# A triangular inverse in a fused two-model kernel: 64x64 blocks against compact 32x32 diagonal blocks

## The chip, the cores and the metric

The kernel runs on 1 core of one Trainium2 chip. It is one program for a whole forward pass; the metric is the device time of one execution in microseconds (us). Its median over three runs is given, and beside it one execution that was profiled.

## The reference, cut to what matters

Two blocks run one after the other on 256 tokens of width 1024: a transformer (two layers) and a recurrent model (two layers of FFN, mixer, FFN). The change lies in the mixer of the second, in the part called RWKV-7:

```python
def step(S, inp):
    r_t, w_t, k_t, v_t, kk_t, b_t = inp
    sa = jnp.einsum('bhvk,bhk->bhv', S, kk_t)
    S = (S * w_t[:, :, None, :]
         - sa[..., :, None] * b_t[:, :, None, :]
         + v_t[..., :, None] * k_t[:, :, None, :])
    return S, jnp.einsum('bhvk,bhk->bhv', S, r_t)
S0 = jnp.zeros((Bn, H, N, N), jnp.float32)
_, ys = lax.scan(step, S0, xs)
```

There are 8 heads of width 64. The kernel does the scan in 4 chunks of 64 tokens. Within a chunk the state's corrections depend on each other through a strictly triangular 64x64 matrix A = (decayed b) times (decayed kk), one for each head and chunk, and what is needed is the inverse of I + A. All of this is float32.

## The kernel before

**Layout.** 8 heads x 4 chunks are 32 small matrices. They lie as 16 units (`UNITS`, four pairs of heads x four chunks) of 64 columns in a tile of 128 partitions x 1024: head h of a pair on partitions 64h to 64h+63. `units(v)` (line 241) is that view. `unit(v, u, h)` is one 64x64 block, and `per_unit(bank, left, right, us)` (lines 2450 to 2455) makes one 64x64 product for each unit and head, into PSUM banks `bank` and `bank + 1`: head 0 uses the array's tile at rows and columns 0 to 63, head 1 the one at 64 to 127.

**The inverse.** `at_` is the masked A transposed, `xs` and `xt` are the growing inverse and its transpose. `xs` and `xt` start as the inverse of 2x2 blocks (masks `low1`, `up1`, then I minus that). Then `LEVELS = [2, 4, 8, 16, 32]` doubles the size of the inverted diagonal blocks five times. A level takes `aoff`, the part of A that joins two neighbouring blocks (mask `lev{m}`, `next_level`, VectorE, line 1701), and on TensorE (lines 2566 to 2580):

```python
per_unit(0, aoff, xs, range(b * 8, b * 8 + 8)).then_inc(lev_p, 1)
for t in gates_at("level", i):
    tile(t, bank=6)
for b in range(2):
    pe.wait_ge(lev_a, LA.at(f"w{b}", step))
    if i < len(LEVELS) - 1:
        per_unit(2, xt, ws, us)
    per_unit(4, ws, xt, us).then_inc(lev_p, 1)
```

The first line is W = A_off X, in two halves of 8 units. ScalarE copies W from PSUM to `ws` (line 1194). X W and its transpose follow, in two halves, and VectorE subtracts them from `xs` and `xt` (line 1817), again by halves. The next level's first half of W waits for the first half's subtraction (`lev_v`), its second half for the second. The last level makes only the product for `xt`, since only `xt` is used afterwards.

**What runs beside it.** `tile(t)` (line 2359) is a column tile of the gate projection: 24 products of 128x128 by 256 columns (lines 2030 to 2032, high and low parts of both operands). `gates_at` places such tiles between the steps: one in each of the first four levels, none in the fifth, then one at the start of each of the four steps of the chunk loop. Its weights come by SP's queue in pairs (`ring_a`, two slots), ScalarE rounds them (`round_t`, line 1012), POOL makes the low part (line 585), and ScalarE empties the result (`empty_gate`, line 1051) and then rounds the tile after next. VectorE does, after each of the first four levels' subtractions, one of four parts of another head normalisation (`standardise`, lines 1799 to 1803).

**Before the inverse.** `per_unit(0, bh, kt)` and `per_unit(2, kt, bh)` (lines 2470, 2471) make A transposed and A in PSUM; VectorE masks them into `at_` and `xs` (`masked`, line 1694), makes `xt` from `at_` (line 1713), and takes both from the identity (lines 1718, 1719). TensorE goes on meanwhile with other products and tiles.

**After it** comes the chunk loop (line 2585 on): for each chunk a product `r` (`sums`, line 2594), a gate tile, the product with `xt` ("u"), VectorE's negation of it (`nu`, line 1875), then state and output. TensorE enters the loop when VectorE has subtracted the last half of `xt`.

The order on each engine is written out by hand, as above; nothing is planned by costs.

## Time and profile before

| | us |
|---|---|
| median of three runs | 2489.09 (2487.69 to 2493.08) |
| profiled execution, its own time | 2488.33 |
| its span, first to last instruction | 2485.8 |
| TensorE busy (matmul) | 2369.6, 95% of the span |
| VectorE, ScalarE, POOL busy | 1449.3, 1047.2, 319.3 |
| mean granted TensorE clock | 0.98 of full speed |

The two layers' inverses lie at 1438.7 to 1481.4 us and 2149.0 to 2191.6 us of the span. TensorE's busy share counts overlapping matmuls once. A clock of 1.00 is 2.4 GHz, 0.50 is 1.2 GHz.

### The profile page before, as it was taken

To read this page: it belongs to the slowest core of one execution; us is meant where nothing else is said; L and a number is where in the kernel's file an instruction comes from. 1 tells how busy PE (TensorE), PEld (TensorE's weight loads), DVE (VectorE), ACT (ScalarE), POOL (GpSimd) and SP (SyncE) were. 2 spreads that over 40 slices of the span, in tenths; PEclk is the share of its full clock that TensorE was granted. 3 is DMA by queue.
4 is the path that set the end of the run, shared out by engine and by line. 5 is a ranking of instruction groups with operands and counts; after the bars stand their busy time and mean duration, and the time that the engine had idled before them with its cause. 6 is when DMAs were issued, how large, how long until landed. Compare 5 with 4: busy or idle time off the path is not lost.

```text
span 2485.8 us, 47529 instructions
## 1 busy us (share of the span) xinstructions
PE 2369.6 (95%) x19164; PEld 2095.1 (84%) x19164; DVE 1449.3 (58%) x2314; ACT 1047.2 (42%) x1666; POOL 319.3 (13%) x263
## 2 busy tenths in 40 slices
PE   7988999999998799999999999999999999999998
PEld 3755899999985599879988888899899888988997
DVE  1053266656625276676667765566666668555665
ACT  3154454454335343343346434433433355435333
POOL 0000000000000000010014435300100125336000
PEclk9999999999999899999999999999999999999999
DMA  6255454544425454355433223654455232124542
GB/s 267 71 198 216 178 191 176 189 169 176 169 85 219 154 203 179 150 178 190 177 106 123 81 72 125 220 189 177 154 189 190 102 138 100 69 87 178 201 179 102
DMA packets 65512, 392.51 MB, mean 158 GB/s; under 512 B 7264, under 2 KB 7392, under 8 KB 28000
## 3 DMA queue, kind: packets, MB, share of 16 engines
q1 hardware_dynamic: 64224, 383.81, 42.3%
q10 hardware_dynamic: 864, 5.16, 0.5%
q8 instruction: 104, 1.70, 0.3%
q0 software_dynamic: 288, 1.57, 0.2%
q14 instruction: 32, 0.26, 0.0%
HBM read 389.46 MB, written 1.05 MB: 157 GB/s over the span
## 4 chain that ended last, share of the span: by engine, by line
PE 82%; DVE 4%; POOL 4%; issue 4%; ACT 3%; DMA 2%; POOLq 0%; SPq 0%; DVEq 0%; ACTq 0%
PE ps L2048 19%; PE ps L2030 11%; PE ps L2031 11%; PE ps L2032 11%; PE ps L2050 10%; PE ps L2139 6%; POOL t_lo L585 3%; PE ps L2154 2%; PE ps L2453 2%; DMA ring_a<-in_wa 2%; PE ps L2594 1%; POOL h_parts L563 1%; PE ps L2000 1%; PE ps L1977 1%; PE ps L2169 1%
## 5 line engine op out<-in xcount | busy, mean ns | idle before, releaser
L2048 PE MATMUL ps<-h_parts,w_hi 128*128 128x512 f32 x2080 | 742.1, 399 | 4.8 <-DVE mod L1258 2.9
L2050 PE MATMUL ps<-h_parts,w_lo 128*128 128x256 f32 x2080 | 584.9, 281 | 0.0
L2048 PEld LDWEIGHTS ps<-h_parts,w_hi 128*128 128x128 f32 x2080 | 391.9, 188 | 96.7 <-DVE mod L1258 3.2
L2050 PEld LDWEIGHTS ps<-h_parts,w_lo 128*128 128x128 f32 x2080 | 394.1, 189 | 0.1
L1330 DVE TENSOR_TENSOR w_lo<-ring_a,w_hi 128x1024 fp32r<-128x1024 f32 x308 | 366.5, 1232 | 24.7 <-ACT w_hi L679 24.5
L2030 PE MATMUL ps<-hid_hi,d_hi 128*128 128x256 f32 x1232 | 349.0, 283 | 0.0
L2031 PE MATMUL ps<-hid_lo,d_hi 128*128 128x256 f32 x1232 | 348.8, 283 | 0.0
L2032 PE MATMUL ps<-hid_hi,d_lo 128*128 128x256 f32 x1232 | 348.6, 283 | 0.0
L711 ACT ACTIVATE sg<-sg 128x256 f32<-128x256 f32 x130 | 54.3, 418 | 655.5 <-DVE sg L1366 655.5
L679 ACT CAST w_hi<-ring_a 128x1024 fp32r<-128x1024 f32 x308 | 305.6, 1040 | 12.3 <-DMA ring_a<-in_wa 12.3
L2030 PE MATMUL ps<-h_parts,t_hi 128*128 128x256 f32 x880 | 260.8, 296 | 17.4 <-POOL t_lo L585 10.6
L1366 DVE TENSOR_REDUCE sg<-ps 128x256 f32<-128x512 f32 x130 | 89.9, 692 | 302.4 <-PE ps L2050 302.4
L2031 PE MATMUL ps<-h_parts,t_hi 128*128 128x256 f32 x880 | 252.8, 287 | 0.0
L2032 PE MATMUL ps<-h_parts,t_lo 128*128 128x256 f32 x880 | 252.5, 287 | 0.0
L563 POOL TENSOR_TENSOR h_parts<-nsq,h_parts 128x256 fp32r<-128x256 f32 x72 | 61.4, 876 | 1435.1 <-ACT h_parts L698 849.3
L2030 PEld LDWEIGHTS ps<-hid_hi,d_hi 128*128 128x128 f32 x1232 | 234.2, 190 | 6.0
L2032 PEld LDWEIGHTS ps<-hid_hi,d_lo 128*128 128x128 f32 x1232 | 234.6, 190 | 0.0
L2031 PEld LDWEIGHTS ps<-hid_lo,d_hi 128*128 128x128 f32 x1232 | 234.5, 190 | 0.0
L585 POOL TENSOR_TENSOR t_lo<-ring_a,t_hi 128x512 fp32r<-128x512 f32 x120 | 172.7, 1463 | 314.6 <-ACT t_hi L1012 314.6
L1337 DVE TENSOR_TENSOR d_lo<-ring_d,d_hi 128x1024 fp32r<-128x1024 f32 x154 | 190.1, 1235 | 11.5 <-ACT d_hi L687 8.9
L2030 PEld LDWEIGHTS ps<-h_parts,t_hi 128*128 128x128 f32 x880 | 172.2, 196 | 25.9 <-issue 13.6
L2031 PEld LDWEIGHTS ps<-h_parts,t_hi 128*128 128x128 f32 x880 | 173.0, 197 | 0.1
(317 smaller groups left out, 3811.7 us busy)
## 6 DMA issues: line engine op xcount, KB each, us to landing
ring_a<-in_wa SPq DMA_DIRECT2D x282, 1024.0 KB, 4.8
ring_d<-in_wd SPq DMA_DIRECT2D x154, 512.0 KB, 5.2
work<-in_wa SPq DMA_DIRECT2D x6, 1024.0 KB, 22.1
work<-in_small POOLq DMA_DIRECT2D x2, 768.0 KB, 5.7
c<-in_c ACTq DMA_DIRECT2D x1, 1175.0 KB, 10.8
work<-in_c ACTq DMA_DIRECT2D x1, 1088.0 KB, 5.0
x<-in_x ACTq DMA_DIRECT2D x1, 1024.0 KB, 15.2
work<-in_ctx ACTq DMA_DIRECT2D x1, 1024.0 KB, 19.6
```

Of the source, the lines that this page charges most:

```text
L563: nc.gpsimd.tensor_tensor(h_lo[:, k, :], nsq[:, k, :], h_hi[:, k, :].bitcast(F32), ALU.subtract)\
L585: nc.gpsimd.tensor_tensor(t_lo[:, t % 2, k], ring_a[:, c % 2, t % 2, k], t_hi[:, t % 2, k].bitcast(F32), ALU.subtract).then_inc(done, 1)
L679: nc.scalar.copy(w_hi[:, f % 2, part], ring_a[:, c % 2, part]).then_inc(hi_a, 1)
L1330: ins = nc.vector.tensor_tensor(w_lo[:, f % 2, part], ring_a[:, c % 2, part], w_hi[:, f % 2, part].bitcast(F32), ALU.subtract)
L1337: nc.vector.tensor_tensor(d_lo[:, f % 2], ring_d[:, d % 2], d_hi[:, f % 2].bitcast(F32), ALU.subtract)\
L1366: nc.vector.reduce_sum(sg[:, f % 2, :], both_parts(bank), AX_X).then_inc(gate_summed, 1)
L2030: nc.tensor.matmul(out, hi, to_hi, start=start, stop=False, skip_group_check=True)
L2031: nc.tensor.matmul(out, hi, to_lo, start=False, stop=False, skip_group_check=True)
L2032: return nc.tensor.matmul(out, lo, to_hi, start=False, stop=stop, skip_group_check=True)
L2048: nc.tensor.matmul(out, w_hi[:, f % 2, part, k, :], h_parts[:, k], start=(k == 0), stop=False, skip_group_check=True)
L2050: mm = nc.tensor.matmul(out[:, 1, :], w_lo[:, f % 2, part, k, :], h_hi[:, k, :], start=False, stop=(k == KD - 1), skip_group_check=True)
L2139: mm = nc.tensor.matmul(ps[:, 4 + p % 2, 0:cols.stop - cols.start], ring_a[:, slot, i % 2, k, :], h[:, k, cols], start=(k == 0), stop=(k = ...
```

## The change

The diagonal blocks of up to 32x32 are now kept compact: 32 partitions x 32 columns for each unit and each quarter of the partitions, so `xs`, `xt`, `aoff` and `ws` use 512 columns instead of 1024 (`xs_h`, `xt_h`, `off_h`, `ws_h`). Four levels (2, 4, 8, 16) run on these, with four 32x32 tiles of the array on its diagonal (`per_half`). The fifth is replaced by one step for the block that lies off the diagonal: `at_far` times `xs_h`, copied by ScalarE, times the far half of `xt`, negated by VectorE (`far_half`, twice). The gate tile of level 16 moves between these two products. The two products before the inverse are split in 32-wide pieces: the diagonal ones for both (`products_near`) and the far one for A transposed only (`products_far`). VectorE's masks shrink; pieces of `xt` are put back in the 64-wide layout after level 16, and `standardise(3)` comes after them. The constants lose 192 of 2,350 columns.

```diff
-LEVELS = [2, 4, 8, 16, 32]
+LEVELS = [2, 4, 8, 16]
+HALF = CHUNK // 2
...
+        def halves_of(v, first):
+            flat = v[:, first:first + 2, :].rearrange("p j t -> p (j t)")
+            return flat.rearrange("p (u t) -> p u t", t=HALF)
+
+        at_h, at_far, xs_h = halves_of(at_, 0), halves_of(at_, 2), halves_of(xs, 0)
+        off_h, xt_h, ws_h = halves_of(aoff, 0), halves_of(xt, 0), halves_of(ws, 0)
...
 ScalarE, levels:
-                        nc.scalar.copy(units(ws)[:, half * 8:half * 8 + 8, :],
-                                       ps[:, half, :].rearrange("p (u t) -> p u t", t=CHUNK)).then_inc(lev_a, 1)
-                    for t in gates_at("level", i):
-                        empty_gate(t)
+                        nc.scalar.copy(ws_h[:, half * 8:half * 8 + 8, :],
+                                       ps[:, half, 0:T].rearrange("p (u t) -> p u t", t=HALF)).then_inc(lev_a, 1)
+                    if i < len(LEVELS) - 1:
+                        empty_gate(gates_at("level", i)[0])
+                act.wait_ge(far_w, l + 1)
+                for h in range(2):
+                    low = slice(h * CHUNK + HALF, (h + 1) * CHUNK)
+                    ins = nc.scalar.copy(ws_h[low], ps[low, 0, :].rearrange("p (u t) -> p u t", t=HALF))
+                ins.then_inc(far_copied, 1)
+                empty_gate(gates_at("level", len(LEVELS) - 1)[0])
...
 VectorE, before the levels:
-                masked(at_, 0, "strict").then_inc(rw_v, 1)
+                masked_half(at_h, 0, "strict_half")
+                for h in range(2):
+                    high = slice(h * CHUNK, h * CHUNK + HALF)
+                    ins = nc.vector.tensor_copy(at_far[high].rearrange("p (b u) t -> p b u t", b=2),
+                                                ps[high, 0:2, T:2 * T].rearrange("p b (u t) -> p b u t", t=HALF))
+                ins.then_inc(rw_v, 1)
                 dve.wait_ge(rw_p, RP.at("a", l))
-                masked(xs, 2, "low1").then_inc(rw_v, 1)
+                masked_half(xs_h, 2, "low1").then_inc(rw_v, 1)
...
+                for h in range(2):
+                    nc.vector.memset(units(xt)[h * CHUNK + HALF:(h + 1) * CHUNK, :, 0:HALF], 0.0)
+                nc.vector.tensor_tensor(xt_h, at_h, each_half("up1"), ALU.mult).then_inc(rw_v, 1)
...
 VectorE, levels:
-                        for buf, bank in ((xs, 2), (xt, 4))[i == len(LEVELS) - 1:]:
+                        for buf, bank in ((xs_h, 2), (xt_h, 4))[:1 if i == len(LEVELS) - 1 else 2]:
                             ins = nc.vector.tensor_tensor(
-                                units(buf)[:, us, :], units(buf)[:, us, :],
-                                ps[:, bank + half, :].rearrange("p (u t) -> p u t", t=CHUNK), ALU.subtract)
+                                buf[:, us, :], buf[:, us, :],
+                                ps[:, bank + half, 0:T].rearrange("p (u t) -> p u t", t=HALF), ALU.subtract)
                         ins.then_inc(lev_v, 1)
+                    if i == len(LEVELS) - 1:
+                        for b in (1, 0):
+                            for h in range(2):
+                                rows = slice(h * CHUNK + b * HALF, h * CHUNK + (b + 1) * HALF)
+                                split = lambda v: v.rearrange("p (b u) t -> p b u t", b=2)
+                                ins = nc.vector.tensor_tensor(
+                                    split(units(xt)[rows, :, b * HALF:(b + 1) * HALF]), split(xt_h[rows]),
+                                    ps[rows, 4:6, 0:T].rearrange("p b (u t) -> p b u t", t=HALF), ALU.subtract)
+                            if b:
+                                ins.then_inc(near_xt, 1)
+                        dve.wait_ge(far_x, l + 1)
+                        for h in range(2):
+                            rows = slice(h * CHUNK, h * CHUNK + HALF)
+                            ins = nc.vector.tensor_scalar(units(xt)[rows, :, HALF:CHUNK],
+                                                          ps[rows, 1, :].rearrange("p (u t) -> p u t", t=HALF),
+                                                          -1.0, None, ALU.mult)
+                        ins.then_inc(xt_whole, 1)
...
 TensorE, before the levels:
+                def products_near(bank, left, right):
+                    for u in range(UNITS):
+                        for h in range(2):
+                            for b in range(2):
+                                row = h * CHUNK + b * HALF
+                                mm = nc.tensor.matmul(ps[row:row + HALF, bank + u // 8, u % 8 * HALF:(u % 8 + 1) * HALF],
+                                                      near(left, u, h, b), near(right, u, h, b), start=True, stop=True,
+                                                      tile_position=(h * HD, row))
+                    return mm
...
-                per_unit(0, bh, kt).then_inc(rw_p, 1)
-                per_unit(2, kt, bh).then_inc(rw_p, 1)
+                products_near(0, bh, kt)
+                products_far(0, bh, kt).then_inc(rw_p, 1)
+                products_near(2, kt, bh).then_inc(rw_p, 1)
...
 TensorE, levels:
+                def per_half(bank, left, right, us):
+                    for u in us:
+                        for g in range(4):
+                            row = slice(g * HALF, (g + 1) * HALF)
+                            mm = nc.tensor.matmul(ps[row, bank + u // 8, u % 8 * HALF:(u % 8 + 1) * HALF],
+                                                  left[row, u, :], right[row, u, :], start=True, stop=True,
+                                                  tile_position=(g * HALF, g * HALF))
+                    return mm
+                def far_half(bank, left, right, to, back):
+                    for u in range(UNITS):
+                        for h in range(2):
+                            k, m = h * CHUNK + back * HALF, h * CHUNK + to * HALF
+                            mm = nc.tensor.matmul(ps[m:m + HALF, bank, u * HALF:(u + 1) * HALF],
+                                                  left[k:k + HALF, u, :], right[k:k + HALF, u, :], start=True, stop=True,
+                                                  tile_position=(k, m))
+                    return mm
...
-                        per_unit(0, aoff, xs, range(b * 8, b * 8 + 8)).then_inc(lev_p, 1)
-                    for t in gates_at("level", i):
-                        tile(t, bank=6)
+                        per_half(0, off_h, xs_h, range(b * 8, b * 8 + 8)).then_inc(lev_p, 1)
+                    if i < len(LEVELS) - 1:
+                        tile(gates_at("level", i)[0], bank=6)
...
-                        if i < len(LEVELS) - 1:
-                            per_unit(2, xt, ws, us)
-                        per_unit(4, ws, xt, us).then_inc(lev_p, 1)
+                        per_half(2, xt_h, ws_h, us)
+                        per_half(4, ws_h, xt_h, us).then_inc(lev_p, 1)
                 pe.wait_ge(lev_v, LV.at("x1", l * len(LEVELS) + len(LEVELS) - 1))
+                far_half(0, at_far, xs_h, 1, 0).then_inc(far_w, 1)
+                tile(gates_at("level", len(LEVELS) - 1)[0], bank=6)
+                pe.wait_ge(far_copied, l + 1)
+                pe.wait_ge(near_xt, l + 1)
+                far_half(1, ws_h, units(xt)[:, :, HALF:CHUNK], 0, 1).then_inc(far_x, 1)
+                pe.wait_ge(xt_whole, l + 1)
```

## Rows read from the trace of the kernel before

**Rows 1.** The page: busy time, and the chain that ended last, by engine
```profile
PE 2369.6 (95%) x19164; PEld 2095.1 (84%) x19164; DVE 1449.3 (58%) x2314; ACT 1047.2 (42%) x1666; POOL 319.3 (13%) x263
...
PE 82%; DVE 4%; POOL 4%; issue 4%; ACT 3%; DMA 2%; POOLq 0%; SPq 0%; DVEq 0%; ACTq 0%
```

**Rows 2.** Windows: length, busy (records) of PE, PEld, DVE, ACT, POOL; PEclk, DMA, GB/s
```profile
1357.95:1361.83 3.88, 3.88 (x129) 3.81 (x128) 3.88 (x3) 3.53 (x6) 3.88 (x2) 1.00 0.02 4
...
1438.69:1481.37 42.68, 40.04 (x994) 38.55 (x993) 26.45 (x35) 15.28 (x22) 12.29 (x10) 1.00 0.18 67
2148.97:2191.64 42.67, 40.03 (x993) 38.54 (x992) 26.45 (x35) 15.28 (x22) 12.30 (x10) 1.00 0.18 65
```

**Rows 3.** Chain of waits, layer 0's inverse: start us, us, what
```profile
1447.76 1.30 DVE work L1817 x2
...
1449.10 1.15 PE ps L2453 x32
1450.24 0.32 PE ps L2030
...
1453.31 3.90 PE ps L2453 x128
...
1458.57 1.15 PE ps L2453 x32
...
1469.20 0.32 PE ps L2030
...
1481.37 0.68 PE ps L2594 x16
```

**Rows 4.** TensorE's timeline: column strips, whole array, 64x64 tiles
```profile
844.01 1.93 PE L1977 MATMUL ps<-ring_a,cs 128*32 128x256 f32 x32
...
1436.87 1.89 PE L2562 MATMUL ps<-work,c 128*128 128x256 f32 x8
...
1443.76 4.88 PE L2453 MATMUL ps<-work 64*64 64x64 f32 x160
```

**Rows 5.** Groups by line: busy us, mean ns of one, idle before
```profile
L1786 DVE TENSOR_TENSOR work<-ps,work 128x256 f32<-128x256 f32 x8 | 3.4, 424 | 0.3
L1194 ACT COPY work<-ps 128x512 f32<-128x512 f32 x20 | 11.5, 586 | 35.8 <-PE ps L2453 35.8
L1012 ACT CAST t_hi<-ring_a 128x1024 fp32r<-128x1024 f32 x94 | 98.0, 1043 | 0.0
```

**Rows 6.** Timeline of VectorE, ScalarE and POOL, layer 0
```profile
1445.44 2.50 POOL L585 TENSOR_TENSOR t_lo<-ring_a,t_hi 128x512 fp32r<-128x512 f32 x2 [4.48 <-ACT t_hi L1012]
...
1453.34 0.38 ACT L1051 ACTIVATE work<-ps 128x256 f32<-128x256 f32 x1 [2.46 <-PE ps L2032]
...
1477.39 1.75 DVE L1799 RECIPROCAL work<-work 128x256 f32<-128x256 f32 x1
1479.17 0.42 DVE L1801 TENSOR_TENSOR work<-work 128x256 f32<-128x256 f32 x1
1479.63 0.49 DVE L1803 SCALAR_TENSOR_TENSOR work<-work,vec 128x256 f32<-128x256 f32 x1
...
1481.50 1.55 DVE L1867 SCALAR_TENSOR_TENSOR work<-work,vec 128x256 f32<-128x256 f32 x4
1485.78 0.42 DVE L1875 TENSOR_SCALAR work<-ps 128x256 f32<-128x256 f32 x1 [2.73 <-PE ps L2594]
```

**Rows 7.** Windows around a drop of the granted clock, layer 0, before the inverse
```profile
1400.40:1406.10 5.70, 5.70 (x17) 4.50 (x17) 1.67 (x3) 4.09 (x6) 0.00 (x0) 0.50 0.00 0
1406.10:1410.10 4.00, 4.00 (x26) 4.00 (x26) 0.56 (x1) 0.00 (x0) 0.00 (x0) 0.69 0.00 0
```

**Rows 8.** The page's DMA parts, and one of TensorE's waits
```profile
q8 instruction: 104, 1.70, 0.3%
...
ring_a<-in_wa SPq DMA_DIRECT2D x282, 1024.0 KB, 4.8
...
PE ps L1977 <- DMA c<-in_c: 3.1, 1, 3.1
```

More of the change, by code:

```diff
@@ L477, in gates_at @@
         def gates_at(what, i):
-            if what == "level" and i == len(LEVELS) - 1:
-                return []
             return [GATES + dict(head=0, mean=4, level=6, chunk=10, y=14)[what] + i]
@@ L2468, in _, with near @@
                     tile(25)
+                def near(v, u, h, b):
+                    j, c = u // NC_, u % NC_
+                    at = c * CHUNK + b * HALF
+                    return v[h * HD:h * HD + HD, j, at:at + HALF]
+                def products_near(bank, left, right):
[7 more added lines that the diff above has]
+                    return mm
@@ new lines, in products_far @@
+                def products_far(bank, left, right):
+                    for u in range(UNITS):
+                        for h in range(2):
+                            row, col = h * CHUNK, T + u % 8 * HALF
+                            mm = nc.tensor.matmul(ps[row:row + HALF, bank + u // 8, col:col + HALF],
+                                                  near(left, u, h, 0), near(right, u, h, 1), start=True, stop=True,
+                                                  tile_position=(h * HD, row))
+                    return mm
```

37 lines of the change are left out of this document (23 added, 14 removed).

## The prediction

> **What bounds the kernel now.** I read the page first. TensorE is busy 95% of the span and carries 82% of the chain that ended last; no other engine has more than 4% of that chain [rows 1]. So what the change takes from TensorE counts, if nothing else ends last in its place. The stretches by window then give the size of the stage: the triangular inverse, from its first product to the first product of the chunk loop, takes 42.68 us in layer 0 and 42.67 in layer 1, with the clock at 1.00 [rows 2]. That is 85.35 us, 3.4% of the span; all else in the diff lies in the 3.88 us of the two products before it. Last I read the chain of waits inside the stage [rows 3]. It repeats: X and XT products (128 records, 3.90 us), the two subtractions of VectorE (1.30), the second half of the next W (32 records, 1.15), one 128x128 gate tile (1450.24 to 1453.31, 3.07), and again, each 9.47 us after the last. The first half of W hides under the subtractions.
>
> **Price of a record.** An f32 product leaves two records: per unit and head one product, so 64 records for 32 products. 160 records of 64 columns take 4.88 us [rows 4], 29.3 ns each once the tail of the last is taken off (4.88 - 0.22 over 159). Two tiles of the array alternate, so each tile takes 58.6 ns for a record. Do tiles really run beside each other? 32 records of 256 columns in four column strips take 1.93 us, and 8 records of the same 256 columns on the whole array take 1.89 [rows 4]: four strips cost what one costs, 216 ns a round ((1.93 - 0.4) / 7). From 256 to 64 columns a tile's record falls by 0.82 ns a column, so at 32 columns it costs 32.4 ns, and with four tiles at once 8.1 ns. That is the low bound. The high bound is 29.3 ns, the fastest that the trace shows records going in over a long burst; nothing shows that records can be fed faster than that for long. I take 9 ns: near the low bound, since the strips show fourfold overlap with the same f32 records, with 10% for start-up and supply. Where only two tiles can work (the products that cross from one half block to the other) I take 16 ns.
>
> The Trainium skill, "TensorEngine Tiling (Array Packing)", section Instruction Overhead, speaks against the change: a small matmul has about 60 cycles of overhead, and one should not tile a dimension that is already small. That would be 25 ns a record if the overhead is the array's. The strips of [rows 4] are too long to show it.
>
> **Records.** Before, the inverse has 96 products on each of four levels and 64 on the fifth: 448, or 896 records a layer. After: four levels of 64 + 64 + 64 products, and two crossing steps of 32: 1,536 records on four tiles and 128 on two. So it has 1.9 times the records at, by my price, under a third of the cost. The two products before the stage go from 128 records to 256 on four tiles and 64 on two.
>
> **The level period after.** W 128 x 9 = 1.15 us; X and XT 256 x 9 = 2.30; the gate tile with its switch 3.17; start-ups 0.1. Then the wait for VectorE: result 0.24, two subtractions. These halve to 256 elements. Such VectorE instructions take 0.42 us, and four in a row 1.55 [rows 5, 6], so two take 0.83 where two of 512 took 1.30; with the release 1.12. The first half of W (0.58) runs inside it, 0.54 is exposed. Period 7.25 against 9.47: 2.2 saved, three times, 6.65. The first W, before the first gate tile, is 128 x 9 = 1.2 for 64 x 29.3 = 1.9 with 0.1 of start: 0.8 saved.
>
> **The end of the stage.** Before: gate tile at 1469.20 to chunk loop at 1481.37, 12.17 us [rows 3]. After, from where that tile would stand: X and XT 2.34; result and one subtraction (xs alone is waited for) 0.71; first crossing step 64 x 16 = 1.05; the moved gate tile 3.17; second crossing step and its result 1.29; two VectorE negations of 512 elements from PSUM, which now end the stage with nothing beside them, 1.33 (two L1817 in 1.30). Sum 9.89: 2.3 saved. ScalarE's two copies of the crossing step (0.59 each, L1194) start when that step ends and are done 1.3 us later, under the tile of 3.1. VectorE's four pieces of xt (4 x 0.61) start with the first crossing step and last 2.5, also under step and tile. Without the tile both would be bare: it is the cover that the move buys. Behind the new waits stand: on TensorE the second crossing step and the chunk loop; on ScalarE the emptying of that gate tile, due 3 us later; on VectorE the negations and all of the next paragraph.
>
> **Moved past queues.** In VectorE's order one of the four parts of the head normalisation stands behind each level: 2.65 us (1.75 + 0.42 + 0.48). With a mask, now of half width (some 0.65), and four subtractions (1.7) that makes 5.0 in a period of 7.25, so VectorE is not the bound. The fourth part used to run at 1477.39 beside TensorE and now stands behind the negations, so it runs as the chunk loop opens: 2.7 + memset + the four of L1867 (1.55) = 4.6 us, and the first nu, which TensorE waits for, came 4.4 us into the loop (1485.78) [rows 6]. I charge 0.35. POOL and ScalarE prepare the gate tiles: 0.38 + 1.04 + 2.50 = 3.9 us after a tile ends the one after next is ready [rows 5, 6]; with periods of 7.25 there are 11 us. The moves of SP's queue are none; a pair of tiles needs one load, 4.8 us to landing, in 14.5 us [rows 8].
>
> **The front.** 128 x 29.3 = 3.8 becomes 256 x 9 + 64 x 16 = 3.3: 0.5 saved. The masks shrink, but two partition-sliced copies of 512 elements come before the release of "at": about 0.6 later than now, and TensorE asks for it 0.5 earlier; that gap is covered by a tile and transposes of 4.1 us except some 0.2. Bounds 0 and 0.6; 0.3 taken. The constants shrink by 192 columns (96 KB) and TensorE waits 3.1 us for that load [rows 8]: 0 to 0.3 us a run, 0.2 taken.
>
> **Sum.** 6.65 + 0.8 + 2.3 - 0.35 + 0.3 = 9.7 a layer, 19.4 for two, with the constants 19.6. Profiled execution 2488.33 - 19.6 = 2468.7; the median of the runs, 2489.09, is 0.8 above it: 2469. Each ns on the price of a record costs some 960 + 256 + 128 + 320 = 1,660 records a layer: 3.3 us for both. At 8.1 ns the time is 2466; the gain is gone at 15 ns.
>
> **Rivals.**
>
> A, supply (the other side): a record is a weight load and a product, so a layer gets 960 x 2 = 1,920 more instructions to feed. If TensorE's queue is fed with one record in 20 ns or more, tiles idle between records. Place: every burst of the levels; it decides from 15 ns. At 22 ns, 13 x 3.3 = 43 more: about 2512, with 2505 at 20 and 2536 at 29.3. For it: no long burst beats 29.3. Against: 58.6 ns is what one tile needs for 64 columns (0.82 a column and some 6 over), so that rate has its own cause, and fetching instructions takes 0.3% of the DMA engines [rows 8]. Chance 0.11.
>
> A2, a fixed cost of each record on the whole array, whatever its columns: same place, same bounds (15 to 29.3 ns), same 2512. Against it, four strips of 256 columns cost no more than one record; for it, they are long enough to hide such a cost. Chance 0.10. By the page named above, whose figure is 25 ns, the time would be about 2522.
>
> B, half supply: bursts start full and then run at 11 to 14 ns (fetches of 16 KB among them). 2476 to 2486. Chance 0.13.
>
> C, the clock: in a stretch where TensorE had gone idle now and then and ran matmuls on 4 rows, the granted clock was 0.50 for 5.7 us, and the next gate tile got it back only midway [rows 7]. After the change a quarter of the array works in the bursts, and waits of 0.5 to 1.6 us follow. If it drops at the end of each stage, tile and crossing steps cost 3 to 4 us more a layer: 2476. Against: with half the array and waits of 0.45 it stays at 1.00 now. Chance 0.10.
>
> D, the array does not overlap row tiles that write one bank, or the waits eat it: no change, 2487 to 2491. The alternation of two tiles in one bank speaks against. Chance 0.04.
>
> Forecast, 2462 to 2475: 0.52.
>
> **Chances.** Two kernels within 0.2% (5 us) can't be told apart here. Faster: 0.52 + 0.09 of B and 0.09 of C and a little from between, 0.71; same 0.08; slower 0.21. The range reaches from 2461 (low bound of the price, front in full) to 2502, and leaves out most of A.
>
> **What would show it.** Bursts of 64 records in 0.6 to 0.8 us; 256 of X and XT in 2.3 (right), 3.8 (the gain is gone), 6 (A). Level period 7.2. Stage 33 us (42.7 less 9.75). Clock 1.00 in it. The gate tile of the last level covers ScalarE's copies. Wait of TensorE for the negations 1.3. First nu 4.7 us into the loop. The forecast is wrong if a four-tile burst costs over 12 ns a record, or if the clock leaves 1.00.

## The result, and the profile after

The kernel got slower: 2547.21 us (median of 4, 2544.61 to 2551.01) against 2491.09 us for the kernel before beside it (2487.69 to 2493.79). The ratio is 1.0226, with a 95% interval of 1.0210 to 1.0243. The forecast was 2469, and its range ended at 2502.

The page after: busy time, the instruction queue (packets, MB, share), and the chain that ended last.

```profile
PE 2383.6 (94%) x21084; PEld 2102.0 (82%) x21084; DVE 1438.4 (56%) x2324; ACT 1044.6 (41%) x1666; POOL 317.5 (12%) x263
...
q8 instruction: 119, 1.95, 0.3%
...
PE 82%; issue 6%; POOL 4%; DVE 4%; ACT 3%; DMA 2%; POOLq 0%; SPq 0%; DVEq 0%; ACTq 0%
```

Beside [rows 1] TensorE has 1,920 records more and only 14 us more busy time, but "issue" (TensorE waits for nothing that the profile shows) rose from 4% to 6% of the chain. Beside [rows 8] the instruction queue has 15 packets more. A record is a weight load and a product: 1,920 records are 3,840 instructions, and 3,840 / 15 = 256 to a packet of 16 KB.

Windows after: the front (from the first product for the triangular matrix to the two products on 4 rows) in layer 0 and 1, and the stage in layer 0 and 1. Columns as in [rows 2].

```profile
1367.36:1394.04 26.68, 23.00 (x601) 22.11 (x601) 19.28 (x23) 9.16 (x16) 11.77 (x7) 0.87 0.21 74
2107.10:2135.21 28.11, 22.94 (x603) 21.96 (x603) 16.05 (x22) 9.38 (x16) 10.67 (x8) 0.88 0.30 107
1454.02:1517.00 62.98, 39.56 (x1761) 37.30 (x1760) 20.07 (x33) 13.55 (x22) 10.93 (x9) 0.73 0.13 46
2191.10:2253.63 62.53, 40.58 (x1761) 38.02 (x1760) 20.07 (x33) 13.78 (x22) 11.05 (x9) 0.73 0.13 46
```

And the front before, in the same two layers:

```profile
1357.95:1378.69 20.74, 20.74 (x410) 20.07 (x409) 20.22 (x19) 9.16 (x16) 12.36 (x7) 1.00 0.27 92
2073.60:2094.35 20.75, 20.75 (x409) 19.95 (x407) 17.04 (x18) 9.29 (x16) 11.72 (x8) 1.00 0.38 142
```

The stage was 42.7 us [rows 2]: it grew by 20.3 and 19.9, the fronts by 5.9 and 7.4. That is 53.5 of the 62.7 us between the two profiled executions (2551.01 and 2488.33). The other 9 stand ahead of the changed levels and products: layer 0's front starts at 1367.36 in place of 1357.95. Two kernels further down, with the same text up to there, start it at 1352.4 (the looped one) and 1353.6 (the one with the 64x64 front), so it is a matter of the execution.

One line of the change, as it is printed ahead, differs from the kernel: `xt_h` is `halves_of(aoff, 2)`, the second half of `aoff`'s buffer, so that its pieces can be put into `xt` without writing over what is still to be read.

TensorE's timeline after, inside the first two levels (start, length, what, idle before and its releaser); pieces of the gate tiles are left out.

```profile
1454.02 1.31 PE L2543 MATMUL ps<-work 32*32 32x32 f32 x128
...
1463.37 1.30 PE L2543 MATMUL ps<-work 32*32 32x32 f32 x123 [2.67 <-issue]
1464.93 0.25 PE L2543 MATMUL ps<-work 32*32 32x32 f32 x4 [0.26 <-DVE work L1844]
1469.69 1.07 PE L2543 MATMUL ps<-work 32*32 32x32 f32 x60 [4.51 <-issue]
...
1471.49 0.41 PE L2074 MATMUL ps<-h_parts,t_hi 128*128 128x256 f32 x1
...
1475.93 1.68 PE L2543 MATMUL ps<-work 32*32 32x32 f32 x172
1479.64 0.54 PE L2543 MATMUL ps<-work 32*32 32x32 f32 x40 [2.03 <-issue]
```

The waits of TensorE in the stage of layer 0 after (total, times, longest), and the same view of before:

```profile
PE ps L2543 <- issue: 19.7, 8, 4.5
PE ps L2553 <- issue: 1.1, 1, 1.1
```

```profile
PE ps L2453 <- DVE work L1817: 1.8, 4, 0.5
```

Read together: a burst runs at 10 ns a record while it runs (128 in 1.31, 123 in 1.30, 172 in 1.68), as forecast. But nine times in the stage of layer 0 TensorE stops in the middle of a burst with no semaphore due, for 20.8 us in all (layer 1: 19.7). Before, no wait for issue stands in the view. Between two stops lie 127 or 128 records, one packet of 256 instructions, or twice that where a gate tile lies between (60 + 24 + 172 records).

The trace also has the start of every packet of the instruction queue. In both layers' fronts and stages TensorE stops 23 times for 0.6 us or more. Each time it goes on 2.2 to 2.7 us after a packet has started. And the next packet starts only after TensorE has gone on into the new block: 1.1 to 1.7 us after in 19 of the 23 cases, 2.7 to 4.2 us in four. So one block is asked for when the block before it is begun, and not earlier, and two blocks can't begin closer than some 1.1 + 2.2 = 3.3 us. The closest pair in a stage is 1479.64 and 1482.96, 3.3 us apart.

And then the clock: the records of a gate tile, 0.28 us each at the upper level (granted 1.00, 2.4 GHz), last 0.41 here, at the lower one (1.2 GHz), and the granted clock of the stage is 0.73, a mixture of both.

These two account for the stage: 42.7, less the forecast gain of 9.7, plus 20.8 of stops, makes 53.8; the 9.2 left to 63.0 are the clock's share. That last term is a remainder. Some 6 us of it can be read: three of the four gate tiles take 5.2, 5.3 and 4.6 us from their start to that of the next burst, for 3.05 before.

### The profile page after: what moved, and what is told of

The parts are those of the page before. It is cut to its first block, busy times and chain, and to the rows that moved or that the text cites. A ratio compares the mean times of both kernels' runs of the same rounds, so it can differ in the third digit from the quotient of the medians.

```text
span 2549.1 us, 51379 instructions
## 1 busy us (share of the span) xinstructions
PE 2383.6 (94%) x21084; PEld 2102.0 (82%) x21084; DVE 1438.4 (56%) x2324; ACT 1044.6 (41%) x1666; POOL 317.5 (12%) x263
## 4 chain that ended last, share of the span: by engine, by line
PE 82%; issue 6%; POOL 4%; DVE 4%; ACT 3%; DMA 2%; POOLq 0%; SPq 0%; DVEq 0%; ACTq 0%
PE ps L2092 19%; PE ps L2074 11%; PE ps L2076 11%; PE ps L2075 11%; PE ps L2094 9%; PE ps L2183 5%; POOL t_lo L595 3%; PE ps L2198 2%; PE ps L2543 1%; PE ps L2690 1%; POOL h_parts L573 1%; DMA ring_a<-in_wa 1%; PE ps L2021 1%; PE ps L2044 1%; PE ps L2213 1%
## 5 line engine op out<-in xcount | busy, mean ns | idle before, releaser
L2074 PE MATMUL ps<-h_parts,t_hi 128*128 128x256 f32 x880 | 267.8, 304 | 18.5 <-POOL t_lo L595 10.7
L2076 PE MATMUL ps<-h_parts,t_lo 128*128 128x256 f32 x880 | 258.7, 294 | 1.4 <-issue 1.4
L2075 PE MATMUL ps<-h_parts,t_hi 128*128 128x256 f32 x880 | 259.2, 295 | 0.0
L2074 PEld LDWEIGHTS ps<-h_parts,t_hi 128*128 128x128 f32 x880 | 179.7, 204 | 28.1 <-issue 15.2
L2075 PEld LDWEIGHTS ps<-h_parts,t_hi 128*128 128x128 f32 x880 | 180.0, 205 | 0.1
```

The costliest lines, as they stand in the source:

```text
L2074: nc.tensor.matmul(out, hi, to_hi, start=start, stop=False, skip_group_check=True)
L2075: nc.tensor.matmul(out, hi, to_lo, start=False, stop=False, skip_group_check=True)
L2076: return nc.tensor.matmul(out, lo, to_hi, start=False, stop=stop, skip_group_check=True)
```

## Experiments

Theory 1 (supply): TensorE's instructions come in blocks of 256 by the instruction queue, and a block takes at least 3.35 us to be there (the two closest packets in the first stage of after start 3.36 us apart). Theory 2 (the array): the small products cost more than 9 ns once many follow. Theory 3 (the clock): it falls first and makes the rest.

### The same products from fewer instructions

```diff
+ def twice_over(us, *products):
+     us = list(us)
+     with pe.Fori(0, 2):
+         for bank, left, right in products:
+             per_half(bank, left, right, us[0:3])
+     for bank, left, right in products:
+         mm = per_half(bank, left, right, us[6:8])
...
- per_half(0, off_h, xs_h, range(b * 8, b * 8 + 8)).then_inc(lev_p, 1)
+ twice_over(range(b * 8, b * 8 + 8), (0, off_h, xs_h)).then_inc(lev_p, 1)
...
- per_half(2, xt_h, ws_h, us)
- per_half(4, ws_h, xt_h, us).then_inc(lev_p, 1)
+ twice_over(us, (2, xt_h, ws_h), (4, ws_h, xt_h)).then_inc(lev_p, 1)
```

The kernel leaves out units 3 to 5 of each half and does units 0 to 2 twice.

> The kernel after, with each burst of the four levels run as a loop that passes twice over the products of three units, with the products of the last two units behind it. As many products as before (8 units to a burst, the same shapes, the same four tiles of the array), but fewer different instructions to bring in: about 546 in place of 830 to a level. Units 3 to 5 of each half are left out (others are done twice), so the inverse isn't the reference's. Theory 1 (supply: PE runs out at every 256th instruction and a block of 256 takes at least 3.35 us to come): 546 instructions are 2.1 blocks, 7.1 us, about the period that was forecast for a level, so a level takes 7.5 to 9 us (four loops to a level may cost 0.1 to 0.3 us each), the stage 34 to 39 us in place of 63, the clock in it goes back to 1.00, and the kernel takes 2470 to 2490 us. Theory 2 (the array: 32x32 products on four tiles cost more than 9 ns in a row of levels): the same products, so the stage stays at 63 us and the kernel at 2547. Theory 3 (the clock falls because of the small products themselves, and that makes the stage long): the clock stays at 0.73 in the stage, the stage above 50 us, the kernel above 2525.

Measured: 2513.49 us, 1.0103 (1.0075 to 1.0131) of before; 34 us below after (31 by the two ratios) with the same 21,084 records. That is over theory 1's range and under theory 3's. Nine instruction packets fewer than after. Windows: up to the second level's first subtraction, the whole stage of layer 0, the stage of layer 1. Then TensorE's waits in the stage of layer 0, and VectorE's subtractions.

```profile
1439.24:1455.05 15.81, 15.10 (x706) 13.30 (x705) 5.37 (x10) 8.37 (x12) 5.13 (x5) 1.00 0.34 108
...
1439.24:1488.06 48.82, 41.16 (x1762) 36.55 (x1761) 19.19 (x33) 13.65 (x22) 10.94 (x9) 0.86 0.18 59
2162.73:2215.63 52.90, 42.45 (x1761) 38.22 (x1760) 19.26 (x33) 13.71 (x22) 10.99 (x9) 0.77 0.15 53
```

```profile
PE ps L2543 <- issue: 3.9, 4, 1.7
PE ps L2699 <- DVE work L1861: 1.5, 1, 1.5
```

```profile
1446.29 0.75 DVE L1844 TENSOR_TENSOR work<-work,ps 128x256 f32<-128x256 f32 x2 [4.11 <-PE ps L2543]
...
1455.05 0.75 DVE L1844 TENSOR_TENSOR work<-work,ps 128x256 f32<-128x256 f32 x2 [3.14 <-PE ps L2543]
```

Stops fell from 20.8 to 3.9 us and the stage by 14.2 in layer 0, from 19.7 to 7.2 and by 9.6 in layer 1: theory 2 is out, since the array has the same to do. The first period is 8.76 us (1446.29 to 1455.05), at a clock of 1.00 and with no stop. A W of 128 records takes 2.18 us here in place of 1.31: 0.43 for each of its two loops. A level has four loops, 1.74 us; without them it would be 7.0, and the forecast said 7.25. So with supply, the forecast's working holds. But the stage was expected at 34 to 39 us and took 49 and 53. Loops account for some 7 of that, stops for 4 and 7, and the clock fell to 0.86 and 0.77 with few stops left.

### Twice the columns, the same instructions

```diff
- mm = nc.tensor.matmul(ps[row, bank + u // 8, u % 8 * HALF:(u % 8 + 1) * HALF],
-                       left[row, u, :], right[row, u, :],
+ mm = nc.tensor.matmul(ps[row, bank + u // 8, u % 8 * HALF:(u % 8 + 2) * HALF].rearrange("p (a t) -> p a t", t=HALF),
+                       left[row, u, :], right[row, u, :][:, None, :].to_broadcast([HALF, 2, HALF]),
                        start=True, stop=True, tile_position=(g * HALF, g * HALF))
```

> The kernel after, with 64 moving columns in place of 32 in every product of the levels (the 32 columns given twice; the second copy lands where the next unit's product overwrites it). The same number of instructions, twice the columns. Theory 1 (supply): a block of 256 instructions is 128 records; even at the 14.7 ns a record that 64 columns would take over four tiles it is worked off in 1.9 us, less than the 3.35 us in which a block comes, so the stage stays within 3 us of 63 and the kernel within 6 us of 2547. Theory 2 (the array is the bound): 5 to 6 ns more for each of 1536 records of a layer, 8 to 9 us a layer, so the kernel takes 2563 or more.

Measured: 2540.21 us, 1.0211 (1.0182 to 1.0240), which overlaps after's 1.0226 (1.0210 to 1.0243). Windows of the two stages, and a burst between stops:

```profile
1440.89:1499.40 58.51, 43.91 (x1762) 41.08 (x1761) 19.30 (x33) 13.64 (x22) 10.95 (x9) 0.88 0.14 49
2177.11:2236.36 59.25, 41.94 (x1761) 39.03 (x1761) 19.36 (x33) 13.64 (x22) 10.94 (x9) 0.94 0.13 49
```

```profile
1445.87 2.98 PE L2543 MATMUL ps<-work 32*32 32x64 f32 x197
1450.30 2.23 PE L2543 MATMUL ps<-work 32*32 32x64 f32 x127 [1.46 <-issue]
```

A record now takes 15 ns (2.98 / 197), and the stage is not longer but 3.3 to 4.5 us shorter, at a clock of 0.88 and 0.94. The array's time isn't the bound. Theory 1 had the stage within 3 us of 63, so it is missed a little, on the side away from theory 2. The stops are shorter (12.6 and 15.4 us for 20.8 and 19.7), as they must be if a block comes at a fixed pace while its records take longer. That the clock would be higher stood in neither theory.

### The loops, with twice the columns

Its edit is the two above together, with the same units left out.

> The kernel with the bursts of the levels as loops that pass twice (fewer different instructions, three units of each half left out and others done twice, so the inverse isn't the reference's), and 64 moving columns in each product of the levels in place of 32. Same instructions, same loops, more array time: 5 ns for each of 1536 records, 7 to 8 us a layer. Theory C1 (the granted clock falls where the products are small in columns, with or without stops of PE; in the looped kernel it fell to 0.86 and 0.77 over the stage with few stops, and to 0.56 over a burst without any in the padded one): the clock of the stage goes up to 0.93 to 1.00, and the longer products are paid back: the stage takes 45 to 52 us, about what it took (49 and 53). Theory C2 (the clock falls because PE stops for instructions, whatever it runs in between): the clock stays at 0.77 to 0.86, and the stage is 7 to 9 us longer than with 32 columns, 56 to 62 us.

Measured: 2506.06 us, 1.0071 (1.0056 to 1.0086).

```profile
1444.37:1490.55 46.18, 42.11 (x1762) 38.56 (x1761) 19.09 (x33) 13.64 (x22) 10.94 (x9) 0.96 0.18 62
2160.35:2210.63 50.28, 43.19 (x1761) 39.55 (x1760) 19.19 (x33) 13.65 (x22) 10.96 (x9) 0.93 0.16 57
```

With the products 50% longer the stage is 2.6 us shorter than in the looped kernel with 32 columns, at 0.96 and 0.93 for 0.86 and 0.77. C2's 56 to 62 us are out, and C1's stage of 45 to 52 us is what came. The stops are shorter too, 2.0 and 4.8 us for 3.9 and 7.2, so the columns aren't all that changed.

### Extra instructions in the kernel before

```diff
  pe.wait_ge(lev_a, LA.at(f"w{b}", step))
+ for _ in range(1):
+     for d in range(96):
+         row = slice(d % 4 * 32, (d % 4 + 1) * 32)
+         nc.tensor.matmul(ps[row, 2 + b, 0:2], const("ident")[row, 0:32], const("ident")[row, 0:2],
+                          start=True, stop=True, tile_position=(row.start, row.start))
```

> The kernel before, with 96 extra products of 2 columns in a straight line ahead of each half of the products for X and its transpose, in levels 0 to 4 of a layer (they write a bank that is overwritten right after; 32 rows, 32 columns of weights, spread over the four tiles; constant operands). Each is 2 records and 4 instructions: 768 more to a level beside some 440. Theory 1 (supply): 1208 instructions are 4.7 blocks of 256, at 3.35 us or more each 15.8 us to a level in place of 9.5: at least 51 us more over the ten levels of both layers (levels 0 to 3; the last one has no gate tile and the same padding, so rather 60 to 70), and more if the clock falls: 2540 to 2590 us. Theory 2 (each record has its price on the array and nothing else counts): 3840 more records of 8 to 10 ns, 31 to 38 us more, 2520 to 2530 us.

The second kernel has `with pe.Fori(0, 2)` over 48 of them:

> As the kernel with 96 extra products ahead of each half, but the 96 are 48 in a loop that passes twice. The same products are executed, and 384 instructions fewer are to be brought in for a level (824, 3.2 blocks, 10.8 us at 3.35 us each, which is less than the 12.6 us or so that the level then takes on the array). Theory 1 (supply): 31 to 38 us over the kernel before for the extra records, and up to 5 for the loops: 2522 to 2535 us, at least 15 us less than the one in a straight line. Theory 2 (a record has its price on the array): the same time as in a straight line within 5 us.

The third has 24 in place of 96:

> The kernel before with 24 extra products of 2 columns ahead of each half of X and its transpose, a quarter of the 96 that cost 109 us. 192 instructions more to a level: 632, 2.5 blocks of 256, 8.3 us at 3.35 each, and the level then lasts some 10.4 us, so the blocks come in time. Theory 1 (supply with a threshold): no stop of PE in the levels, only 960 records more at 10 ns: 8 to 13 us over the kernel before, 2498 to 2503. Theory 2 (an added record costs the same whatever the number, 109 / 4): 27 us more, 2517. Theory 3 (the clock: small products lower it at any dose): the clock of the stage below 0.95 and 15 us more or above.

Measured: 2598.77 us in a straight line (1.0437, 1.0410 to 1.0464), 2557.44 looped (1.0281, 1.0252 to 1.0310), 2504.40 with 24 (1.0066, 1.0042 to 1.0090). TensorE's timeline in the straight line of 96:

```profile
1451.12 1.96 PE L2453 MATMUL ps<-work 64*64 64x64 f32 x59 [1.77 <-issue]
1453.02 0.74 PE L2581 MATMUL ps<-c 32*32 32x2 f32 x69
1454.86 1.19 PE L2581 MATMUL ps<-c 32*32 32x2 f32 x123 [1.10 <-issue]
1455.98 0.41 PE L2453 MATMUL ps<-work 64*64 64x64 f32 x5
1458.59 1.65 PE L2453 MATMUL ps<-work 64*64 64x64 f32 x26 [2.20 <-issue]
```

59 + 69 and 123 + 5 records: 128 each, whatever their kind, and they start 3.74 and 3.73 us after one another. That is the rate of supply here, 29 ns a record; the shortest distance seen, the 3.3 us in the stage of after, is 26. The whole is over theory 1's 2540 to 2590 as well. TensorE waits for issue for 18.8 us in the stage of layer 0. The looped kernel executes the same 23,004 records with 15 packets fewer and is 41 us faster: theory 1, and the array's price is out as the reason for the stops. Its waits for issue in the stage of layer 0 sum to 1.1 us. Yet it is 68 us over before, where 31 to 38 were expected. Its windows (both stages, then a padding burst with the X products behind it), and the timeline there:

```profile
1434.81:1508.23 73.42, 69.31 (x2914) 65.42 (x2913) 26.65 (x35) 15.27 (x22) 12.24 (x10) 0.86 0.12 40
...
1445.21:1454.26 9.05, 9.05 (x323) 8.89 (x321) 3.78 (x5) 0.58 (x1) 0.00 (x0) 0.57 0.33 117
```

```profile
1445.21 2.89 PE L2581 MATMUL ps<-c 32*32 32x2 f32 x192
1448.04 6.22 PE L2453 MATMUL ps<-work 64*64 64x64 f32 x128
```

TensorE is busy without a break for 9.05 us, and the granted clock is 0.57. 128 records of X and its transpose, 3.90 us in [rows 3], take 6.22. The clock fell to its lower level at 1442.8, in the burst behind two runs of small products with one stop of 0.31 us between them, and came back at 1453.1. So it can be down where TensorE doesn't stop; what makes it fall isn't shown. Theory 3 names a second cause and not the first, since the straight line loses 41 us more with the same products.

With 24, two stops (0.8 us) stand in the stage of layer 0, the clock is 1.00, and the stage takes 49.86 us. It cost 16.6 us over before (2487.84 beside it): somewhat over theory 1's 8 to 13, which had no stop, and well under the 27 of a price that stays the same. An added record costs 17 ns with 24 products and 28 with 96. So the cost rises faster than the dose, as it does when the blocks come in time at first and then don't.

### The front as it was

```diff
...
- products_near(0, bh, kt)
- products_far(0, bh, kt).then_inc(rw_p, 1)
- products_near(2, kt, bh).then_inc(rw_p, 1)
+ per_unit(0, bh, kt).then_inc(rw_p, 1)
+ per_unit(2, kt, bh).then_inc(rw_p, 1)
...
+ for g in range(4):
+     rows, col = slice(g * HALF, (g + 1) * HALF), g % 2 * HALF
+     ins = nc.vector.tensor_tensor(
+         dst[rows].rearrange("p (b u) t -> p b u t", b=2),
+         ps[rows, bank:bank + 2, :].rearrange("p b (u t) -> p b u t", t=CHUNK)[:, :, :, col:col + HALF],
+         const(mask)[rows, None, None, :].to_broadcast([HALF, 2, 8, HALF]), ALU.mult)
```

> The kernel after with the products in front of the levels as they were (64x64 blocks, two of the array's tiles, 64 products of each kind) and the compact blocks cut out of the bank by VectorE, with four instructions of 32 partitions in place of one of 128 for each of the two masks. 384 instructions fewer for PE in a layer, some 4 us more for VectorE. Theory 1 (supply, also ahead of the levels: two stops of PE, 1.9 and 2.2 us, stand there in the trace of after, and that stretch takes 26.7 us in place of 20.7): the stops go, the granted clock of the stretch is back at 1.00, and since VectorE was busy for 20.2 of 20.7 us before, the stretch is as long as VectorE makes it: 22 to 25 us; the stage of the levels stays at 59 to 63 us; the kernel takes 2533 to 2545. Rival (the six microseconds come from the order of VectorE's work in the new front): the stretch is no shorter than 26 us and the kernel takes 2547 or more.

Measured: 2527.05 us, 1.0163 (1.0144 to 1.0183).

```profile
1353.60:1375.90 22.30, 20.88 (x410) 20.10 (x410) 21.75 (x25) 9.19 (x16) 11.82 (x7) 1.00 0.23 79
2087.40:2108.10 20.70, 20.70 (x409) 20.05 (x408) 19.23 (x27) 9.12 (x16) 11.28 (x8) 1.00 0.39 137
1434.83:1494.91 60.08, 38.91 (x1761) 36.37 (x1760) 20.06 (x33) 13.54 (x22) 10.93 (x9) 0.74 0.14 49
2162.95:2227.60 64.65, 40.23 (x1761) 37.63 (x1760) 20.07 (x33) 13.63 (x22) 10.94 (x9) 0.71 0.13 44
```

The fronts lose their stops (2.0 and 1.7 us in layer 0 of after) and are back at 1.00: 4.4 and 7.4 us shorter. The stages stay long (their sum is 124.7 us for 125.5). The fronts explain 12 us. By the two ratios the kernel gained 16, and their intervals leave that uncertain by some 5, so nothing else has to be found. (The medians alone are 20 apart, and the kernel lies below the 2533 that was expected, but they were taken beside different runs of before.)

### The off-diagonal step alone

The kernel before, levels 2 to 16 as they were, level 32 as in the change:

```diff
+ far_half(0, units(at_)[:, :, HALF:CHUNK], units(xs)[:, :, 0:HALF], 1, 0).then_inc(far_w, 1)
+ tile(gates_at("level", len(LEVELS) - 1)[0], bank=6)
...
+ far_half(1, units(ws)[:, :, 0:HALF], units(xt)[:, :, HALF:CHUNK], 0, 1).then_inc(far_x, 1)
```

> The kernel before with one part of the change alone: the levels 2 to 16 stay in 64x64 blocks on two tiles, and level 32 is the off-diagonal step (product of 32x32 quadrants, copy under the gate tile that is moved there, second product, negated copy). The number of PE's instructions stays about the same (a product of level 32 for a product of the step). Worked out from the rows of before: the level of 16 loses its gate tile (3.1 us) and gains a wait for ScalarE's copy of 1 us, the step has 64 records at 16 ns, the tile, 64 records, and 1.4 us for the negations, and the stage ends within 0.5 us of where it ended. Theory 1 (supply is the only thing that failed): 2489 us within 4, no stop of PE in the stage. Rival (the step has a wait of its own that the forecast missed): 5 us more or worse for both layers.

Measured: 2489.68 us, 0.9998 (0.9984 to 1.0013): no difference. The stages take 41.92 and 41.90 us, with no stop. This part does what it was meant to and, alone, is worth nothing that can be measured.

### Versions meant to beat both

First, 64x64 weights with 32 moving columns for W and X:

```diff
- per_unit(0, aoff, xs, range(b * 8, b * 8 + 8)).then_inc(lev_p, 1)
+ compact(0, aoff, xs_c, range(b * 8, b * 8 + 8)).then_inc(lev_p, 1)
...
  tile(gates_at("level", i)[0], bank=6)
...
+     mm = compact(2, xt, ws_c, range(b * 8, b * 8 + 8))
+ mm.then_inc(lev_p, 1)
+ pe.wait_ge(ws_wide, step + 1)
+ per_unit(4, ws, xt).then_inc(lev_p, 1)
...
  pe.wait_ge(ch_a, step + 1)
+ if c == 0:
+     pe.wait_ge(xt_whole, l + 1)
  sums(narrow(1), [(here(xt), here(rr))]).then_inc(ch_p, 1)
```

> A version meant to beat both: built on the kernel before. The weights stay 64x64 blocks with zeros beside the two 32x32 blocks, so the number of products and of PE's instructions stays as before (64 for W, 64 records each), but the moving operand of W and of X is compact (32 columns), the transposed product keeps 64. ScalarE writes W twice, compact and wide, under the gate tile; level 32 is the off-diagonal step, its negations covered by the first sums and the gate tile of the chunk loop; the whole inverse is computed. Theory 1 (with the supply as before, the array's time counts, and half the moving columns are half of it): W 64 records 1.05 us in place of 1.9, X the same, transposed product 1.9: a level in 7.1 us in place of 9.5, the stage 32 to 36 us in place of 42.7, the kernel 2468 to 2478 us; no stop of PE on a 256th instruction. Rival A (loading 64x64 weights sets the price, not the columns that move): W and X stay at 29 ns a record, the stage 38 to 41 us for the covered negations and the shorter subtractions alone, 2482 to 2488. Rival B (the clock: fewer columns in the levels, and it falls below 0.9 in the stage): stage 38 to 46 us, 2480 to 2500.

Measured: 2483.14 us, 0.9985 (0.9972 to 0.9997): 0.15% faster than before, just clear of the noise.

```profile
1457.30 2.05 PE L2508 MATMUL ps<-work 64*64 64x32 f32 x64
1459.18 2.06 PE L2488 MATMUL ps<-work 64*64 64x64 f32 x64
```

```profile
1443.07:1482.34 39.27, 37.81 (x993) 36.78 (x992) 21.25 (x27) 22.43 (x38) 12.25 (x10) 1.00 0.21 73
```

Half the moving columns take the same 2.05 us, and stage (39.27 in both layers) and time lie where rival A has them; theory 1 is out. With 64x64 weights the moving columns don't set a record's price at this size; I take it that the load does. What is left is the order: both halves of X first, then both of its transpose, and the negations under the chunk loop's first work. It gives 42.68 - 39.27 = 3.4 us a stage, 6.8 for two, and the medians differ by 6.8. The second version keeps that order with all operands wide (edit against the first version, with VectorE's and ScalarE's part left out):

```diff
- compact(0, aoff, xs_c, range(b * 8, b * 8 + 8)).then_inc(lev_p, 1)
+ per_unit(0, aoff, xs, range(b * 8, b * 8 + 8)).then_inc(lev_p, 1)
...
- mm = compact(2, xt, ws_c, range(b * 8, b * 8 + 8))
+ mm = per_unit(2, xt, ws, range(b * 8, b * 8 + 8))
```

> A simpler version meant to beat both: 64x64 blocks throughout as in the kernel before, all operands wide (64 moving columns), with the order of the kernel with compact moving operands: both halves of X first, then both of the transposed product, so that the subtraction for the next W runs beside the transposed product; a gate tile in each of the four levels; level 32 as the off-diagonal step; its negations covered by the first sums and the gate tile of the chunk loop. Theory (the moving columns cost nothing: W's 64 records took 2.06 us with 32 of them and 1.93 with 64, and what made the kernel with compact operands faster is its order alone): the stage 38.5 to 40 us in place of 42.7, the kernel 2480 to 2486. Rival (half of the moving columns did give a part): 2486 to 2490.

Measured: 2486.56 us, 0.9987 (0.9970 to 1.0003), stages of 39.12 and 39.67 us: as short as with compact operands, so the order made the gain in the stage. The whole kernel can't be told from before, nor from the first version: the ratios are 0.9987 and 0.9985, and most of the 3.4 us between the two medians lies between the kernels before that ran beside them (2487.84 and 2489.97). The third puts W of the first version on four tiles:

```diff
- compact(0, aoff, xs_c, range(b * 8, b * 8 + 8)).then_inc(lev_p, 1)
+ quarters(0, aoff, xs_c, range(b * 8, b * 8 + 8)).then_inc(lev_p, 1)
```

> The kernel with compact moving operands, with W alone on four tiles: 32x32 weights, 128 products of it to a level in place of the 32 of 64x64 (as each product is two records: 128 records in place of 64). 128 instructions more to a level: some 570, 2.2 blocks, 7.5 us at 3.35 each, in a level of 8.0 us. Theory 1 (below the supply's rate four tiles pay, at it the bursts stall): W in 1.3 us in place of 2.06 where no block ends in it; where a block falls mostly into a burst of W, a stop of up to 2 us: the stage 36.5 to 40 us, the kernel 2476 to 2486. Rival (small products cost by themselves, in clock or in a fixed price): the stage above 42 us, the kernel above 2490.

Measured: 2495.65 us, 1.0031 (1.0016 to 1.0046): 0.3% slower than before. Stage and time lie where the rival has them (above 42 and 2490), yet by stops, which theory 1 named.

```profile
1438.81:1482.71 43.90, 37.08 (x1249) 35.19 (x1249) 22.45 (x27) 22.45 (x38) 12.27 (x10) 0.97 0.18 65
```

```profile
1457.44 1.13 PE L2516 MATMUL ps<-work 32*32 32x32 f32 x107
1460.55 0.38 PE L2516 MATMUL ps<-work 32*32 32x32 f32 x21 [1.98 <-issue]
```

W was to save 0.75 us a level; this stop in the middle of a burst costs 2.0, and the waits for issue in the stage of layer 0 sum to 4.7 us, where the first version has none. The stage is 4.6 longer, so nothing of W's gain is left; the clock's share (0.97) isn't taken apart from it. An average rate below the supply's isn't enough: a burst of 128 records is a whole block in 1.3 us, and the next one can't be there.

## Why the prediction was wrong

**The failed step** is rival A's dismissal: "Against: 58.6 ns is what one tile needs for 64 columns ..., so that rate has its own cause, and fetching instructions takes 0.3% of the DMA engines". The first half was true and the second says nothing: what counts is how long one packet takes to be there, not its share of 16 engines. The sum had no term for it beyond "10% for start-up and supply" in the 9 ns. The runs show 3.3 to 3.7 us for 256 instructions, 26 to 29 ns a record, and 20.8 and 19.7 us of stops in the two stages. 29 ns is just where the kernel before ran, by chance: right after a stop, with a new block there and the clock at 1.00, 59 of the same 64x64 records took 1.96 us in the padded kernel, 30 ns each with the tail of the last taken off. The gate tiles between its bursts gave it slack. The change asked for 1.9 times the records.

The demand could have been counted from [rows 8] and [rows 1]; the time of a block could not be read from a stage without stops. 104 packets are few, but the question was how many fall into 9.47 us. A level before has 192 records and a gate tile's 24, 432 instructions or 1.7 blocks, 6.2 us at 3.7. After it has 384 and 24, 816 or 3.2 blocks, 11.8 us, against a forecast period of 7.25. The Trainium skill, "Advanced Engine Details and Errata", section ISA Cache, has the block: 256 instructions to a line of 16 KB, and only two lines. The packets here agree with the first, 3,840 / 15 = 256, and that no packet starts before the block ahead of it is begun fits the second. But the same section of the Trainium skill gives TensorE 128 KB, by estimate eight such lines, and no run here tells the two apart. The time of a line is this case's.

Rival A had the right side and mechanism, but its place, "every burst of the levels; it decides from 15 ns", supposed a slower burst. A burst is not slower; it stops at a block's end. By its own formula 29 ns would give 2536, and the clock adds to that; 2547 was measured.

**The clock.** Rival C expected it to fall after waits, at the end of each stage, for 3 to 4 us a layer. It was 0.73 over the whole stage, and from 1465.4 on at the lower level by turns (some 9 us a layer as a remainder, 6 of them read from the gate tiles); in the fronts it was 0.87 and 0.88. It was down without waits as well: 0.57 over 9.05 us in which TensorE was never idle (padded and looped kernel).

**Point by point.** The price of 9 ns a record: 10 ns while a burst runs, right within its bounds. Rival A2, a fixed cost on the whole array: wrong, four tiles overlap. The Trainium skill, "TensorEngine Tiling (Array Packing)", section Instruction Overhead, has about 60 cycles for a matmul, which as an overhead of the whole array would by estimate be 25 ns a record; the trace's 128 in 1.31 us don't agree with that. Reading of the strips: (1.93 - 0.4) / 7 is 219 ns a round and not 216, which moves the low bound of 8.1 by 0.1. Two tiles at 16 ns: 64 records of the second crossing step took 1.20 us, 19 ns, at a clock of 1.00. Level period 7.25: 7.0 where supply and clock allow, with the loops taken off. Wait for the negations 1.3: 1.5. The constants, 0.2: the wait for them went from 3.1 to 2.9. Stage 33: 63. Two negations 1.33: 1.38. The fourth part of the normalisation behind them: so. The first nu 4.7 us into the loop, at 1517.00: 4.5. These rows show the last three:

```profile
1515.57 1.38 DVE L1861 TENSOR_SCALAR work<-ps 32x512 f32<-32x512 f32 x2 [6.22 <-PE ps L2553]
1516.98 1.75 DVE L1826 RECIPROCAL work<-work 128x256 f32<-128x256 f32 x1
...
1521.48 0.42 DVE L1919 TENSOR_SCALAR work<-ps 128x256 f32<-128x256 f32 x1
```

The front, 0.3 saved: 5.9 and 7.4 lost, by the same cause (3.7 and 5.2 us of stops, the rest at a clock of 0.87 and 0.88). The crossing step, part of the 2.3 saved at the end: by itself the stage gains 0.8 us and the kernel nothing.

**Not settled.** What made the clock fall. The stages had 0.73 with 20.8 and 19.7 us of stops and 32 columns, 0.86 and 0.77 with 3.9 and 7.2 us and 32 columns, 0.88 and 0.94 with 12.6 and 15.4 us and 64, 0.96 and 0.93 with 2.0 and 4.8 us and 64. It goes neither by the stops alone nor by the columns alone, and no run takes the two wholly apart.

The longest stop (4.51 us) is the one before which the packet was late: TensorE had begun a block at 1463.37, and the next packet started 4.1 us later. In all four of the 23 cases with such a delay, over 2 us, a weight load was moving meanwhile; of the 19 others only two had one. No run varies the load, so it stays argued that the load is the reason. In the DMA engines' slices of 1465.2 to 1469.7 the load's traffic ends at about 1467.1, and only then does the one instruction packet of that stretch come, 146 GB/s in one slice.

```profile
DMA  9699993995998958900050000000000000000000
GB/s 437 291 437 437 437 728 146 437 583 218 510 437 364 655 218 364 437 0 0 0 146 0 0 0 0 0 0 0 0 0 0 0 0 0 0 0 0 0 0 0
...
q8 instruction: 1, 0.02, 1.3%
```

## What to carry to other kernels

Before cutting matmuls into smaller ones, count TensorE's instructions in the busiest few microseconds (a record is two; an f32 product of these levels is two records, four instructions), divide by 256, and compare with 3.3 to 3.7 us a block: straight-line code was not fed faster here, whatever the array would do. A price below 26 to 29 ns a record is only of use in bursts that are short beside a block; to gain over a longer stretch, the instructions must get fewer (larger products, or a loop whose body stays loaded). And where small products fill a stretch, look at the granted clock in it: here it was 0.73, and the large products between them paid too, 5.2 us a gate tile for 3.05.

## What had not been expected of the hardware

- Stops of TensorE 128 f32 records apart, or twice that, each of 0.6 to 4.5 us, in straight-line code; the packet that ends a stop starts at the earliest 1.1 us after the block before it is begun.
- With 32x32 weights on four tiles a record took 9 ns with 2 moving columns (192 in 1.77 us, padded kernel), 10 with 32 and 15 with 64; with 64x64 weights on two tiles it was 32 ns (2.05 / 64) for either.
- A loop of two passes costs 0.43 us over the same products in a row (0.3 in the padded kernels: 192 records in 2.09 us for 1.77).
- The granted clock was 0.57 over 9.05 us in which TensorE's records show it busy without a break, and a stage got shorter (63 to 59 us) by doing twice the columns.
